# Residual additions of tiles 1 to 3 on VectorE, ten rows of tile 0 per half projection, two query jobs ahead of tile 1, routing at a step's front

## What is computed

```
h = rmsnorm(x);  u, v, q, k, v' = h @ w_in
x = x + concat(gmlp(u, v), dilated_attention(q, k, v')) @ w_out
# PEER: 8 heads, 16 of 16384 experts per head and token
qq = rmsnorm(x) @ w_q;  s = qq . sub_keys            # two halves of 128 keys per head
top 16 of each half -> top 16 of the 256 sums -> expert numbers eid, gates g
hid = gelu(einsum(u_tab[eid], rmsnorm(x)))
x = x + einsum(g * hid, v_tab[eid]);  y = rmsnorm(x)
```

## Time and profile before

| | us |
|---|---|
| median of three runs | 1708.4 |
| lowest, highest | 1699.86, 1709.84 |
| span of the profiled execution, first to last instruction | 1709.3 |

### The profile page before, as it was taken

How to read it: one execution, slowest core, us unless ns; L and a number is a source line. 1 busy time by engine, 2 the same in 40 slices (tenths; PEclk the granted TensorE clock), 3 DMA queues, 4 the chain that set the end, 5 groups by cost and what they waited for, 6 DMA issues and landing times.

```text
span 1709.3 us, 17753 instructions
## 1 busy us (share of the span) xinstructions
PE 1404.9 (82%) x5164; PEld 622.7 (36%) x5164; DVE 1085.5 (64%) x2884; ACT 634.5 (37%) x1889; POOL 652.7 (38%) x703
## 2 busy tenths in 40 slices
PE   8999996768997978888878887777777777777786
PEld 5585663435333434334423232222223222222211
DVE  2459978868000046777766766666668888888654
ACT  2421113445211024344444454444445444444443
POOL 3034333322565653333333333333333333333332
PEclk9999996888998989999999999999999999999999
DMA  9798889999999999999999999999999999999997
GB/s 344 292 357 313 318 318 364 398 411 385 358 362 338 386 375 399 413 409 417 410 423 421 406 416 422 421 421 403 407 422 396 414 422 420 405 419 413 409 406 324
DMA packets 112144, 664.81 MB, mean 389 GB/s; under 512 B 13072, under 2 KB 14336, under 8 KB 52400
## 3 DMA queue, kind: packets, MB, share of 16 engines
q0 software_dynamic: 97824, 571.75, 83.4%
q1 hardware_dynamic: 14224, 91.93, 13.8%
HBM read 658.03 MB, written 5.60 MB: 388 GB/s over the span
## 4 chain that ended last, share of the span: by engine, by line
DMA 37%; PE 37%; issue 8%; ACT 7%; DVE 6%; another core or an unknown queue 3%; POOL 0%; ACTq 0%; SPq 0%; DVEq 0%; POOLq 0%
DMA area_r<-in_uv_tab,eid 36%; PE bank L907 11%; PE bank L627 9%; PE bank L851 4%; PE bank L896 4%; ACT area_c L1003 3%; PE bank L798 2%; DVE area_r L1703 2%; PE bank L558 1%; PE bank L871 1%; ACT L1253 1%; DVE area_x L1711 1%; DMA area_w<-in_w_in 1%; PE bank L767 1%
## 5 line engine op out<-in xcount | busy, mean ns | idle before, releaser
L907 PE MATMUL bank<-area_r,area_c 128*128 128x512 f32 (+1 forms) x1584 | 778.8, 624 | 213.8 <-ACT area_c L1003 212.8
L1873 POOL DMA_INDIRECT area_r<-in_uv_tab,eid x544 | 515.7, 948 | 944.0 <-PE bank L907 590.0
L1703 DVE CUSTOM_DVE_ANT_0 area_r<-area_r,bank 128x1024 f32<-128x1024 f32 x416 | 506.3, 1218 | 288.0 <-DMA area_r<-in_uv_tab,eid 287.3
L907 PEld LDWEIGHTS bank<-area_r,area_c 128*128 128x128 f32 (+1 forms) x1584 | 273.3, 188 | 713.0 <-issue 712.6
L1253 ACT ACTIVATE area_c<-hid 128x1 f32<-128x1 f32 x416 | 84.2, 202 | 538.8 <-DVE hid L1703 538.3
L1694 DVE CUSTOM_DVE_ANT_0 area_r<-area_r,bank 128x1024 f32<-128x1024 f32 x128 | 152.9, 1212 | 25.5 <-DMA area_r<-in_uv_tab,eid 22.7
L627 PE MATMUL bank<-area_w,area_t 128*128 128x384 f32 (+1 forms) x448 | 157.6, 509 | 4.1 <-DMA area_w<-in_w_in 3.5
L1003 ACT ACTIVATE area_c<-ident,area_c 128x128 f32<-128x128 f32 x364 | 146.1, 401 | 34.9 <-ACT area_c L1003 1.1
L1873 POOL DMA_INDIRECT area_r<-in_uv_tab,eidT x128 | 121.4, 948 | 82.0 <-issue 29.3
L1003 ACT ACTIVATE area_x<-bank 128x384 f32<-128x384 f32 (+8 forms) x123 | 49.9, 423 | 212.4 <-remote 59.4
L851 PE MATMUL bank<-area_t,area_w 128*128 128x416 f32 (+1 forms) x448 | 118.8, 418 | 6.1 <-issue 5.2
(11 more groups left out here) (200 smaller groups left out, 1202.6 us busy)
## 6 DMA issues: line engine op xcount, KB each, us to landing
area_w<-in_w_in SPq DMA_DIRECT2D x12, 1536.0 KB, 11.1
area_w<-in_k_cache SPq DMA_DIRECT2D x8, 1920.0 KB
area_w<-in_w_q SPq DMA_DIRECT2D x14, 1024.0 KB, 6.8
area_r<-in_uv_tab,eid POOLq DMA_INDIRECT x544
area_w<-in_w_out SPq DMA_DIRECT2D x4, 2048.0 KB, 11.6
area_w<-in_v_cache SPq DMA_DIRECT2D x4, 1920.0 KB
area_v<-in_v_cache SPq DMA_DIRECT2D x4, 1152.0 KB
area_x<-in_x_p SPq DMA_DIRECT2D x6, 512.0 KB
```

Source lines behind the costliest of these rows:

```text
L907: mm = pe.matmul(acc[0:n, c, :], diag[by_pe(i) % DG][:, 0:n], x_ring[s][:, D + c * 512:D + (c + 1) * 512], start=(i == 0), stop=False, ski ...
L1703: vec.tensor_tensor_reduce(out=u, in0=u, in1=x_cur, scale=1.0, scalar=0.0, op0=ALU.mult, op1=ALU.add, accum_out=hid[t % 2][:, j:j + 1]).th ...
L1873: nc.gpsimd.indirect_dma_start(out=ring[s], out_offset=None, in_=table, in_offset=bass.IndirectOffsetOnAxis(ap=where, axis=0)).then_inc(la ...
```

## The change

- `project_out` for tiles 1 to 3 ends without the identity matmul. A new function `add_x_late` on VectorE waits for `x_tile[t]` and each half's end, and adds the half from PSUM into `x_tile[t]`; ScalarE's `read_out` stays for the sample tile only.
- `project_out` takes two counts: tokens of tile 0 weighed amid it and after it. They are 4 and 6 for tiles 1 to 3 (before 4 and 4), 4 and 4 for the sample tile.
- `JOBS_AHEAD` is 2, not 3. Each of the two jobs ahead has four more tokens weighed between its queries and its key scores. `BY_DVE` so covers six heads, 24 slots, not 20; six jobs are made within tile 1. Their parts come after slots 1, 6 and 11 rather than 3, 8 and 13.
- Routing: step 8 routes nothing; steps 9 to 14 route the next step's head (before, the one after it), two pieces after each dot from slot 0 on; step 15 routes heads 16 and 17. From step 16 on it is as before. In tile 1 `exp_head` comes at slot 10 (before 1) and `finish_head` at slot 13 (before 3).
- SP loads `gain` ahead of the later query weights.

```diff
-ROUTE_STEP = {g: [g + 2] for g in range(8, 24)} | {g: [2 * g - 22, 2 * g - 21] for g in range(24, 31)}
+ROUTE_STEP = ({g: [g + 1] for g in range(9, 15)} | {15: [16, 17]} | {g: [g + 2] for g in range(16, 24)}
+              | {g: [2 * g - 22, 2 * g - 21] for g in range(24, 31)})
-JOBS_AHEAD = 3
+JOBS_AHEAD = 2
...
-            i, p = HEADS + JOBS_AHEAD + j // TOPK, {3: 0, 8: 1, 13: 2}.get(j % TOPK)
+            i, p = HEADS + JOBS_AHEAD + j // TOPK, {1: 0, 6: 1, 11: 2}.get(j % TOPK)
...
+            sp.wait_ge(xn_ready, NT)
+            sp.dma_start(gain[:], gains[2:3, :].broadcast_to([P, D])).then_inc(gain_in, 16)
             for i in range(HEADS + 3, len(JOBS)):
                 sp.wait_ge(q_done[1], i - 2)
                 load_wq(wq_ring[(i - HEADS) % 3], JOBS[i][0], wq_again[(i - HEADS) % 3])
-            sp.wait_ge(xn_ready, NT)
-            sp.dma_start(gain[:], gains[2:3, :].broadcast_to([P, D])).then_inc(gain_in, 16)
...
-            def project_out(t, c, tokens=0):
+            def project_out(t, c, amid=0, after=0):
...
                     if k == KD // 2:
-                        weigh_first(tokens)
+                        weigh_first(amid)
                     if t < SAMP:
                         mm = pe.matmul(ps[0:n, :], featT[:, k, a:a + n], w(k, c * 512, (c + 1) * 512),
-                                       start=(k == 0), stop=False)
+                                       start=(k == 0), stop=(k == KD - 1))
...
+                if t == SAMP:
+                    pe.wait_ge(x_in[t], 32)
+                    for g, (lo, hi) in enumerate(OUT_COLS):
+                        mm = pe.matmul(ps[CG * g:CG * g + n, 0:hi - lo], ident[0:n, 0:n],
+                                       x_tile[t][0:n, c * 512 + lo:c * 512 + hi], start=False, stop=True)
                 mm.then_inc(out_done, 1)
-                weigh_first(tokens)
+                weigh_first(after)
...
-            project_out(1, 1, 4)
+            project_out(1, 1, 4, 6)
             for t in range(2, NT + 1):
                 if t < NT:
-                    project_out(t, 0, 4)
-                    project_out(t, 1, 4)
+                    for c in range(2):
+                        project_out(t, c, 4, 6 if t < SAMP else 4)
                 turn_xn(t - 1)
                 weigh_first(4)
             pe.wait_ge(xnT_ready, 2 * NT)
             pe.wait_ge(x2_ready, 2 * NT)
-            queries(HEADS, 4)
-            for i in range(HEADS + 1, HEADS + JOBS_AHEAD):
+            for i in range(HEADS, HEADS + JOBS_AHEAD):
                 queries(i, 4)
-                key_scores(i - 1)
-            key_scores(HEADS + JOBS_AHEAD - 1)
+                weigh_first(4)
+                key_scores(i)
...
+            def add_x_late(t):
+                n = TILES[t][1]
+                dve.wait_ge(x_in[t], 32)
+                for c in range(2):
+                    dve.wait_ge(out_done, 2 * t + c + 1)
+                    xh = x_tile[t][0:n, c * 512:(c + 1) * 512]
+                    vec.tensor_tensor(xh, xh, half(4 + c)[0:n, :], ALU.add).then_inc(x2_ready, 1)
...
             for t in range(1, NT):
+                if t < SAMP:
+                    add_x_late(t)
                 norm_x2(t)
...
-                        if i == 3 and HEADS + 2 <= g + 1 < HEADS * SAMP:
+                        if i == (13 if t == 1 else 3) and HEADS + 2 <= g + 1 < HEADS * SAMP:
                             finish_head(g + 1)
...
-                        if i >= TOPK - LINKS - 1:
+                        if t == 1 and len(ks) == 1:
+                            go_on(links, 2)
+                        elif i >= TOPK - LINKS - 1:
                             go_on(links, len(ks))
```

## The result

The changed kernel takes 1719.76 us (median of 20 runs), the kernel before, on the same chip in the same session, 1710.09 us (20 runs). The ratio is 1.0052 with a 95% interval of 1.0036 to 1.0067: slower by half a per cent. The forecast was 1700 us with a range of 1688 to 1711: both the sign and the range were wrong, though "within 1%" holds for the ratio. The profiled execution of after has a span of 1711.3 us; up to the start of tile 0's v rows it happened to be some 10 us quicker than that of before, in work that the change doesn't touch. So stretches are compared here, not spans.

The account below looks back on a forecast made before the run. It took the kernel as waiting for memory (413 GB/s), with time to gain only at 440 to 660 us. -12 + 0.4 + 3 = -8.6 us on the 1709.3 us span gave 1700.7, so 1700 us; range 1688 to 1711.

Parts of the forecast that it names:

- The price of the placement: Tile 1's steps: slots 2, 3, 7, 8 wait up to 5.2 us, the ring's slack covers it; 3 us, bounds 0 and about 10.
- Rival 3: Tile 1's ring runs dry, each delayed pair costing two slots of 2.54 us in six steps: 30 us, 1726 us; chance 0.07.
- The gain of the transition: Stretch from 460 us to the hand-over to tile 1: 12 us of lost DMA time come back, bounds 0 and 22.8.
- Half projections of 12.7 us with bursts of 3.6 us: `project_out` of tiles 1 to 3: 11.87 - 0.96 + 1.8 = 12.7 us, with six-row bursts of 3.6 us.
- TensorE and DMA are then balanced: Half projections with ten rows: 5.24 MB in 12.7 us, so 413 GB/s instead of 353.
- of 6.9 us in 460 to 510, 6: 460 to 510 us, `project_out` of tiles 2 and 3: 6 of 6.9 us of lost DMA time come back, about 410 GB/s.
- Rival 2: Nothing arrives: earlier-requested rows only wait longer, the sample's stretch and unattributed stalls set the pace, tile 1 costs; 1708 us, chance 0.18.
- TensorE reaches its last-but-one stage at 606.6, the routing starts about 607.5: Before tile 1: TensorE's stage moves from 618.96 to 606.6 us, VectorE's routing from 624.07 to about 607.5.
- Seventh gather of tile 1 at 627 to 633: Start of tile 1: seventh gather, 643.73 us before, at 627 to 633; by TensorE alone 17.5 us sooner, at 626.
- Of 4.9 us at the hand-over, 3: 630 to 660 us, gathers of tile 1 start earlier: 3 of 4.9 us of lost DMA time come back, near 413 GB/s.
- Residual additions: VectorE, tiles 1 to 3: six additions of 0.6 to 1.3 us each, hidden; six identity matmuls (5.8 us) leave TensorE.
- The sixth job, the denser routing, `gain`: Tile 1: 0.4 us for the sixth in-loop job, 0 for routing, 0 for loading `gain` earlier (bounds 0 and 1.9 gain).

Follow-up runs that it names:

- 14: The changed kernel with only the first half query early (parts after slots 1, 8, 13): 1711.10 us against 1711.35 for the kernel before, ratio 1.0005.
- 15: The changed kernel with only the second half query early (parts after slots 3, 6, 13): 1706.99 us, ratio 0.9962 to the kernel before.
- experiment 1: The changed kernel with the query parts of tile 1 back after slots 3, 8 and 13: 1705.51 us against 1714.53 for the kernel before, ratio 0.9949.
- experiment 2: The kernel before with only the query parts of tile 1 moved to after slots 1, 6 and 11: 1720.62 against 1714.53 us, ratio 1.0044.
- 3: The kernel before with only tile 1's routing changed, two pieces after each dot from slot 0 on: 1710.57 us, ratio 0.9986.
- 10: The changed kernel with parts after slots 3, 8, 13, eight rows per half projection and identity matmuls, leaving the job count: 1708.40 against 1711.63 us, ratio 0.9973.
- experiment 6: The kernel of experiment 1 with eight rows of tile 0 per half projection again, not ten: 1701.72 us, ratio 0.9949 to the kernel before.
- 11: The kernel of experiment 1 with head 9 routed in step 8 and eight rows per half projection: 1701.99 us, ratio 0.9945 to the kernel before.
- 12: The kernel before with only the residual additions of tiles 1 to 3 on VectorE instead of identity matmuls: 1705.90 us, ratio 0.9973.
- experiment 7: The kernel of experiment 1 with the residuals of tiles 1 to 3 back on TensorE's identity matmuls and ScalarE's copies: 1705.70 us, ratio 0.9976 to the kernel before.
- experiment 13: The kernel of experiment 1 with every second half-projection matmul of tiles 1 to 3 left out (sums wrong): 1700.43 against 1711.35 us for the kernel before, ratio 0.9955.
- 5: The kernel of experiment 1 with head 9 routed in step 8, not ahead of the first dot: 1702.22 against 1711.03 us for the kernel before, ratio 0.9947.
- 8: The changed kernel with the query parts of tile 1 one slot later, after slots 2, 7 and 12: 1716.67 us, ratio 1.0038 to the kernel before.
- 9: The changed kernel with the slots that VectorE adds moved by two, to 2, 3, 7 and 8: 1712.91 against 1711.63 us for the kernel before, ratio 1.0006.

## Why the prediction was wrong

**The price of the placement, the term that decided.** The prediction named the place: slots 2, 3, 7 and 8 now wait on TensorE behind a half query. It named the yardstick too: the slack of the ring lies between 2.7 and 7.7 us against a delay of up to 5.2 us. It then took the middle of the two bounds, found that 5.2 us "just holds", and put 3 us. The failed step is the middle. In after a gather issued some 7 us behind the one before it finds few others ahead, and where VectorE waits for it, the start of its dot product is its landing. For the gathers of slot 8 of the first six steps this takes 5.6 to 7.9 us; the longest is shown above, the shortest is this one (GpSimd, VectorE):

```profile
772.73 0.94 POOL L1887 DMA_INDIRECT area_r<-in_uv_tab,eid  x1 [6.36 <-PE bank L909]
...
778.29 1.22 DVE L1713 CUSTOM_DVE_ANT_0 area_r<-area_r,bank 128x1024 f32<-128x1024 f32 x1 [0.47 <-DMA area_r<-in_uv_tab,eid]
```

The trace of before has the same in the third gather of the earlier trace rows, issued at 633.30, 8.0 us behind the second: its dot product starts at 638.76, 5.5 us later. None comes near the 2.54 us of the transfer. So of the usual 10.2 us only the queue in front can be saved, 2.3 to 4.6 us, which is below the 5.2 us taken; and the batch holds TensorE for 5.75 us, not 5.2. The delay exceeds the slack by some 1 to 3.5 us per batch (an estimate from these numbers); the job stretches give 1.5 us a step for the first batch and 0.8 for the second (experiments 14 and 15).

The Trainium skill, "DMA: Bandwidth & Descriptors", section "Anatomy of one DMA — SWDGE (gpsimd) path", fits the time of such a transfer as 2.0 us plus the bytes at 436 GB/s; an estimate by it is 2.0 + 2.4 = 4.4 us for 1.05 MB. The trace does not agree: 5.6 to 7.9 us here, counted to the dot product. By the page the slack would have been 5.8 us, more than a delay of 5.2 us; the measurement decides.

Rival 3 was this mechanism, with a chance of 0.07 and a price of 30 us: two slots of 2.54 us in six steps. Measured are 15.4 us in the job stretch, 2.6 us a step, and 18 us in the medians: the right mechanism, at half the price. Its threshold, 2 us per step, was right; its sign, windows of tile 1 below 395 GB/s, was too strict (397 and 400, where the forecast was 405 to 412). Its "against" (VectorE and TensorE lag side by side) was wrong: GpSimd needs the places in order, and the longest single wait counts.

**The gain of the transition.** Forecast 12 us, bounds 0 and 22.8. The kernel of experiment 1, without the placement, gains 0.51%, 8.7 us. The forecast for it is 11.6 us (12 less 0.4 for the sixth job), so the size is not far off. But the gain does not come as the working had it.
- Half projections of 12.7 us with bursts of 3.6 us: right for tile 2; those of tile 3 take 13.6 and 14.6 us (477.68 to 491.24 to 505.82). There bursts of four rows take 2.6 and 3.3 us, not 1.87, which points to rows that landed late. Tile 2 (TensorE's timeline of after, first batch of a half, its second batch, and the next half):

```profile
446.01 3.70 PE L799 MATMUL bank<-area_w,area_t 128*128 128x512 f32 x8
...
451.51 3.70 PE L799 MATMUL bank<-area_w,area_t 128*128 128x512 f32 x8
...
458.73 3.70 PE L799 MATMUL bank<-area_w,area_t 128*128 128x512 f32 x8
```

- "TensorE and DMA are then balanced" at 413 GB/s, and "of 6.9 us in 460 to 510, 6": too much. The window has 359 GB/s, not 410. Sixty row sets (thirteenth to 73rd) take 89.1 to 90.3 us with eight rows and identity matmuls (before, 2, 3, 10), 87.3 to 88.5 with eight rows and no identity matmuls (6, 11, 12) and 85.6 to 86.9 in all ten kernels with ten rows; the means are 89.6, 87.9 and 86.3. So the two edits do shorten this stretch, by 3.3 us together, which is less than half of the 8 us forecast for 460 to 560. With ten rows the identity matmuls no longer matter (experiment 7: 85.6), nor does half of the others (experiment 13: 85.8). Row sets of 4 KB can come faster: 401 GB/s in 440 to 460 of after and 396 in experiment 13, where nearly all bytes are such sets, and 400 in 560 to 630 of before, of which a ninth are query weights. Why not in all of the stretch was not found. Rival 2 had a part of this; but its "DMA share 0.95 to 1.0 already" says little, as a share of 0.96 goes with 359 GB/s and one of 1.02 with 401 in the table of after.
- "TensorE reaches its last-but-one stage at 606.6, the routing starts about 607.5": in after the routing of head 9 starts at 610.79 (VectorE's timeline below), 171.7 us behind the thirteenth row set; before, 624.07 - 450.93 = 173.1. Forecast was 16.6 us sooner, measured 1.4. One part is the wait for ScalarE at the first key scores, 4.3 us (experiment 13), which the working did not have there. For the rest, 122 row sets must have landed before those key scores, 120 before the change. At the 1.45 us a set that this stretch has, the sets alone take the time, and what the removed job frees goes into waiting for rows; this is argued from the pace, no run shows it alone.

```profile
610.79 0.49 DVE L1557 MAX8 rt<-area_w 128x8 f32<-128x128 f32 x2 [19.46 <-issue]
```

- "Seventh gather of tile 1 at 627 to 633": it is at 628.84, but by luck, as the thirteenth row set came 11.8 us earlier than in before. Behind that set the seventh gather comes 3.1 us sooner, not 17.5.
- "Of 4.9 us at the hand-over, 3": 330 GB/s in 630 to 660 is no better than before (346); the early half query stands behind the first slots of tile 1 as well.

Of the 0.27% each for the residual additions and the job count the traces show only the former, with 1.7 us in the sixty row sets (means of 89.6 and 87.9): behind them one execution scatters more than the medians differ. That the two together are real rests on the medians; that they are worth 4 to 5 us each is an estimate from intervals that reach zero.

**Residual additions.** Forecast 0.6 to 1.3 us each, hidden. Measured 688 ns (VectorE's groups of after, 430 to 560 us), hidden: right.

```profile
L1543 DVE TENSOR_TENSOR area_x<-area_x,bank 128x512 f32<-128x512 f32 x6 | 4.1, 688 | 68.1 <-PE bank L799 50.9 <-remote 9.5 <-issue 7.7
```

**The sixth job, the denser routing, `gain`.** Forecast 0.4, 0 and 0 us. Experiments 10 and 3 agree for the first two within their intervals. In after the start of `finish_y(0)` has no wait for gain (711.22, where the earlier trace rows has 1.90 us); that place of `gain` follows from the six jobs in the loop, since `finish_y(0)` would otherwise wait for a load queued behind later jobs' weights, and it was not tried alone.

**The sum with measured terms.** Residual -4.6, job count -4.6, ten rows 0, routing 0, placement +18: +8.8 us, against +9.7 us between the medians. The placement term is itself taken from after and experiment 1, so the sum tests only that the other four make the -8.7 us of experiment 1; by experiment 2 the placement would be +7.5. The best kernels are those of experiments 1, 5, 6 and 11, all at 0.9945 to 0.9949; experiment 6 is the simplest, the change without its early parts and without the ten rows.

## What to carry to other kernels

Where a long batch is put into a loop fed by a ring, place it where the next ring places are freed by another engine, and compare the longest interval between two issues with what the ring holds in flight, not the mean load of the engines. The slack of a ring is the queue in front of a transfer, not the whole time from issue to landing: take the shortest landing that the trace has (5.5 us in before, so a slack of 4.7), and when a term hangs on slack with wide bounds, price it at the bad end. An engine that is busy all of the time need not be what holds a stretch up once a little is taken off it: leave out a part of its work and see.

## What the runs showed of the hardware that was not expected

- Gathers of 128 rows of 4 KB each: over sixty sets they came at 1.43 to 1.5 us a set in all seventeen kernels, 348 to 367 GB/s, though shorter stretches of such sets reach 396 to 401 GB/s; with 8 KB rows the DMA engines move 412 to 416 GB/s at a share of 1.01. Their share over 460 to 510 us is 0.96 to 0.98 in before, after and experiments 1 to 12, at 347 to 373 GB/s. Whether the twelve-place ring, GpSimd (0.94 us per issue, at best one each 1.24 us) or something else holds the slower parts was not told apart.
- A gather of 1.05 MB issued 6.9 to 7.3 us behind the one before it took 5.6 to 7.9 us to the start of its dot product; the transfer is 2.54 us at 413 GB/s.
- In nine of the twelve kernels with two jobs ahead TensorE waited 4.0 to 7.9 us for ScalarE's first copy of the key scores, with no cause in the profile; behind the wait of after (4.3 us) the DMA engines fell to 139 GB/s.
- Up to the thirteenth row set, executions of programs that are the same there took between 439 and 451 us (after and experiments 1, 5, 8, 9, 14, 15): a scatter as large as the effects studied, so single spans decide nothing here.
